# In-projection of a decoder layer: seven block products for eight, in two column groups

## What is computed

```python
x = layer_norm(...)                      # (1024, 1024)
u = x * (1.0 + sc2) + sh2
h = u @ w_in[l]                          # D_IN = 1976 columns
q_a, kc, vc, ksl, vsl, kwn, vwn, gate_logits, cq, ckv, k_rope = jnp.split(h, split_at, axis=-1)
```

## Time and profile before

| | |
|---|---|
| time, three executions | 2159.4, 2165.7, 2170.2 us; median 2165.7 |
| profiled execution | 2163.7 us, span from first to last instruction 2162.0 us |
| in-projection | first transpose at 693.6 us, last product starts at 886.5 us |
| TensorE busy in the span | 95% |
| mean granted TensorE clock | 0.983 of 2.4 GHz |

### The profile page before, as it was taken

One profiled execution on the slowest core, in us unless ns is written; L12 is line 12 of the kernel. 1 busy time (PEld: TensorE's weight loads), 2 busy tenths in 40 slices (PEclk: granted clock), 3 DMA queues, 4 the chain that ended last, 5 costly groups with the idle time before them and its releaser, 6 DMA issues. The chain is left out here.

```text
span 2162.0 us, 28296 instructions
## 1 busy us (share of the span) xinstructions
PE 2064.4 (95%) x10049; PEld 1725.5 (80%) x10049; DVE 1518.0 (70%) x2342; ACT 983.4 (45%) x1893; POOL 755.4 (35%) x702
## 2 busy tenths in 40 slices
PE   5999999999999999889998899999999999999997
PEld 4788888877887888778787888778888888878885
DVE  6877777868688523679988678765655555558689
ACT  3433233334644321578878467634533333234443
POOL 0366556620200000167555135401145655630201
PEclk9999999999998999999999999999999999999999
DMA  7254554457941332010000000042233233348975
GB/s 276 88 175 158 175 174 155 159 176 250 297 155 46 107 119 72 6 42 1 1 1 1 1 1 1 30 156 89 87 108 108 92 118 103 127 153 257 299 245 97
DMA packets 195710, 254.38 MB, mean 118 GB/s; under 512 B 20271, under 2 KB 118639, under 8 KB 195574
## 3 DMA queue, kind: packets, MB, share of 16 engines
q1 hardware_dynamic: 180166, 208.04, 29.0%
q0 software_dynamic: 15408, 44.57, 8.0%
HBM read 212.72 MB, written 43.52 MB: 119 GB/s over the span
## 5 line engine op out<-in xcount | busy, mean ns | idle before, releaser
L2993 POOL TENSOR_TENSOR nsa_exps<-nsa_exps,nsaa_factor 128x512 f32<-128x512 f32 (+1 forms) x102 | 96.3, 973 | 91.9 <-DVE nsaa_factor L2980 91.9
L758 DVE TENSOR_TENSOR ffn2A_u<-ffn2A_u,ffn_banks 128x512 f32<-128x512 f32 x60 | 41.2, 687 | 116.6 <-PE ffn_banks L702 112.5
L1292 DVE SCALAR_TENSOR_TENSOR late_part_late<-ada_rows,far_silu_c,late_part_late 128x1024 f32<-128x1024 f32 x56 | 107.1, 1912 | 3.4 <-DMA ada_rows<-in_w_ada 3.3
L579 ACT ACTIVATE ffn1A_t_hi<-ffn1A_t 128x512 fp32r<-128x512 f32 x80 | 48.5, 628 | 132.8 <-POOL ffn1A_t L572 102.9
L579 ACT ACTIVATE ffn2A_t_hi<-ffn2A_t 128x512 fp32r<-128x512 f32 x80 | 48.4, 628 | 122.8 <-POOL ffn2A_t L572 93.7
L702 PE MATMUL ffn_banks<-ffn1S_s_hi,ffn1A_t_hi 128*128 128x512 f32 x240 | 93.8, 391 | 0.0
L702 PE MATMUL ffn_banks<-ffn1S_s_hi,ffn1A_t_lo 128*128 128x512 f32 x240 | 93.4, 389 | 0.0
L702 PE MATMUL ffn_banks<-ffn1S_s_lo,ffn1A_t_hi 128*128 128x512 f32 x240 | 93.4, 389 | 0.0
L702 PE MATMUL ffn_banks<-ffn2S_s_hi,ffn2A_t_hi 128*128 128x512 f32 x240 | 93.4, 389 | 0.0
L702 PE MATMUL ffn_banks<-ffn2S_s_lo,ffn2A_t_hi 128*128 128x512 f32 x240 | 93.4, 389 | 0.0
L702 PE MATMUL ffn_banks<-ffn2S_s_hi,ffn2A_t_lo 128*128 128x512 f32 x240 | 93.4, 389 | 0.0
(11 more groups left out here) (660 smaller groups left out, 7034.6 us busy)
## 6 DMA issues: line engine op xcount, KB each, us to landing
ada_rows<-in_w_ada POOLq DMA_DIRECT2D x56, 512.0 KB, 4.7
ffn_raw_g<-in_ffn_wg SPq DMA_DIRECT2D x44, 512.0 KB, 3.7
ffn_raw_u<-in_ffn_wu SPq DMA_DIRECT2D x44, 512.0 KB, 5.0
early_w<-in_w_ada SPq DMA_DIRECT2D x16, 512.0 KB, 7.2
mix_in_w_raw<-in_w_in SPq DMA_DIRECT2D x32, 247.0 KB, 2.7
ffn_rest<-in_ffn_wd SPq DMA_DIRECT2D x29, 256.0 KB, 5.0
hidden<-ffn1A_c SPq DMA_DIRECT2D x22, 256.0 KB, 4.5
hidden<-ffn1A_u SPq DMA_DIRECT2D x22, 256.0 KB, 5.0
```

Source lines behind the costliest of these rows:

```text
L579: act.activation(self.b_hi[w][:, :], self.block_of(w), ACT.Copy).then_inc(self.rounded, 1)
L758: dve.tensor_tensor(out, base, bank, ALU.add).then_inc(self.mixed, 1)
L1292: dve.scalar_tensor_tensor(out=part_late[:, v, :], in0=ada[:, n % 2, :], scalar=silu_c[:, k:k + 1], in1=part_late[:, v, :], op0=ALU.mult, ...
L2993: pool.tensor_tensor(at, at, by, ALU.mult).then_inc(self.weighed, 1)
```

## The change

The product is cut into two column groups, 0 to 1303 (group 0) and 1304 to 1975 (group 1), and in each group rows, columns and depth are halved: 512 rows, 652 or 336 columns, depth 512. The four blocks of the result come from seven block products for eight. With a the four blocks of `u` and b those of the weight, the left operands are a11, a12, s1 = a21 + a22, s4 = a12 - s2, s2 = s1 - a11, s3 = a11 - a21, a22; the right ones are b11, b21, and differences of pieces. Products `m2`, `m3`, `m7`, `m4` go on in the banks of the product before them (`IN_JOINS`), which are read to `h` first and not cleared.

There are 14 stages (product, group), numbered 0 to 13, each of four chunks, numbered 0 to 55 through all stages: stage 0 is chunks 0 to 3. A group 0 chunk is 4 row tiles x 3 products x 2 halves of 326 columns; a group 1 chunk is 4 x 3 products of 336 columns. The weight pieces are 326 KB and 168 KB. There are four raw buffers (`RAWS`) and three slots of split weights (`PARTS`). `m5` loads two pieces a chunk and blends them once, `m6` three pieces and two blends, `m7` and `m4` one and one; all blends are GpSimd's. ScalarE reads the banks of stages 0 to 3, VectorE those of stages 4 to 13 and adds what is in `h`. The 64 one-column instructions of the modulation sums stand ahead of chunk 0. The residual rows, their stores, the 2 MB loads (`ahead`, in front of chunks 31 and 37) and the rotary rows are spread over the chunks. The diff, cut to its core:

```diff
+KH = DC // 2
+IN_GROUPS = ((0, COL_CQ // 2), (COL_CQ, (D_IN - COL_CQ) // 2))
+IN_STAGES = (("m1", 1), ("m2", 1), ("m1", 0), ("m2", 0), ("m5", 0), ("m3", 0), ("m5", 1), ("m3", 1),
+             ("m6", 0), ("m7", 0), ("m4", 0), ("m6", 1), ("m7", 1), ("m4", 1))
+IN_LEFT = {"m1": "a11", "m2": "a12", "m5": "s1", "m3": "s4", "m6": "s2", "m7": "s3", "m4": "a22"}
+IN_JOINS = ("m2", "m3", "m7", "m4")
+IN_PIECES = {"m1": ((0, 0),), "m2": ((1, 0),), "m5": ((0, 1), (0, 0)), "m3": ((1, 1),), "m6": ((1, 1), (0, 1), (0, 0)),
+             "m7": ((0, 0),), "m4": ((1, 0),)}
+IN_BLENDS = {"m1": 0, "m2": 0, "m5": 1, "m3": 0, "m6": 2, "m7": 1, "m4": 1}
+RAWS, PARTS = 4, 3
...
+        def piece_free(eng, r):
+            q, j = pieces[r]
+            name = chunks[q][1]
+            if name == "m6":
+                eng.wait_ge(blended, blends_before[q] + (1 if j == 1 else 2))
+            elif j == 1:
+                eng.wait_ge(blended, blends_before[q] + 1)
+            else:
+                eng.wait_ge(split, q + 1)
...
         @block.sync
+            def load(q):
+                _, name, g, c = chunks[q]
+                for j, (kh, nh) in enumerate(IN_PIECES[name]):
+                    r = piece_no[q, j]
+                    if r >= RAWS:
+                        piece_free(sp, r - RAWS)
+                    first = IN_GROUPS[g][0] + nh * width(g)
+                    sp.dma_start(piece(q, j), src[:, kh * KH + c, first:first + width(g)]).then_inc(landed[r % RAWS], 16)
...
+            for q in range(RAWS, len(chunks)):
...
+                for i in stores.get(q, ()):
+                    store(i)
+                if q == 31:
+                    sp.wait_ge(x_out, 16 * TT)
+                    ahead(sp, 0)
+                if q == 37:
+                    ahead(sp, 1)
+                load(q)
...
         @block.gpsimd
+            def mix(q):
+                _, name, g, c = chunks[q]
+                if not IN_BLENDS[name]:
+                    return
+                for j in range(len(IN_PIECES[name])):
+                    piece_landed(pool, q, j)
+                p0 = piece(q, 0)
...
+                elif name == "m6":
+                    pool.tensor_tensor(p0, p0, piece(q, 1), ALU.subtract).then_inc(blended, 1)
+                    if q == KH * in_stage("m6", 0):
+                        wait_used(pool, KH * in_stage("m5", 1) + KH - 1)
+                    pool.wait_ge(blended, blends_before[q] + 1)
+                    pool.tensor_tensor(t2(g, c), p0, piece(q, 2), ALU.add).then_inc(blended, 1)
...
         @block.scalar
+            def weight(q):
+                _, name, g, c = chunks[q]
+                if IN_BLENDS[name]:
+                    act.wait_ge(blended, blends_before[q + 1])
+                else:
+                    piece_landed(act, q, 0)
+                if q >= PARTS:
+                    wait_used(act, q - PARTS)
+                act.activation(b_hi[:, q % PARTS, 0:width(g)], product(q), ACT.Copy).then_inc(hi_ready, 1)
...
+            unit(8)
+            take(0)
+            unit(9)
...
+            unit(14)
+            unit(15)
+            weight(9)
+            take(1)
+            weight(10)
...
         @block.vector
+            grown_at = {15: 3, 17: 4, 20: 5, 21: 6, 23: 7}
+            rope_at = {39: (0,), 40: (1,), 43: (2,), 44: (3,), 47: (4,), 49: (5,), 51: (6,), 53: (7,)}
+            for q in range(11, len(chunks)):
+                if q >= KH * 4 + 6 and (q - 6) % KH == 0:
+                    take((q - 6) // KH)
+                if q in sums_at:
+                    sums(sums_at[q])
+                for name, c in low_at.get(q, ()):
+                    sum_low(name, c)
+                weight(q)
+                if q in grown_at:
+                    grow(grown_at[q])
+                for i in rope_at.get(q, ()):
+                    turn_rows(i)
+            take(len(IN_STAGES) - 1)
...
         @block.tensor
+            def rows(q):
+                n, name, g, c = chunks[q]
+                a = IN_LEFT[name]
+                pe.wait_ge(split, q + 1)
...
+                for t in range(KH):
+                    if c == 0:
+                        bank_free(n, t)
+                    tile = slice(t * P, (t + 1) * P)
+                    for m, (ua, wb) in enumerate(((0, b_hi), (0, b_lo), (1, b_hi))):
+                        for b in range(2 - g):
+                            bank, n_cols = (t, width(1)) if g else (2 * t + b, edge // 2)
+                            last = pe.matmul(acc[:, bank, 0:n_cols], part(a, ua, c)[:, tile],
+                                             wb[:, q % PARTS, b * n_cols:(b + 1) * n_cols],
+                                             start=(name not in IN_JOINS and c == 0 and m == 0), stop=(c == KH - 1 and m == 2),
+                                             skip_group_check=True)
```

More of the change, by code:

```diff
@@ new lines, in project_in @@
+        landed = [s.sem(f"landed{k}") for k in range(RAWS)]
+        blended, hi_ready, split, used, row_done = (s.sem(x) for x in ("blended", "hi_ready", "split", "used", "row_done"))
+        taken_act, taken_dve = s.sem("taken_act"), s.sem("taken_dve")
+        s1_made, s3_made, s2_made, s4_made = (s.sem(x) for x in ("s1_made", "s3_made", "s2_made", "s4_made"))
+        sum_hi, sum_split = s.sem("sum_hi"), s.sem("sum_split")
+        rows_in, scaled, grown = s.sem("rows_in"), s.sem("scaled"), s.sem("grown")
@@ L1891, in _, with rows_of, row_parts @@
+        def rows_of(i, cols, g):
+            at = out[:, i, cols]
+            return at.rearrange("p (b n) -> p b n", b=2) if g == 0 else at
+        def row_parts(i):
+            return x_sb[:, i, :].rearrange("p (b n) -> p b n", b=4)
+        row_gain, row_offset = (out[:, 4 * k:4 * k + 4, IN_GROUPS[1][0] + width(1):IN_GROUPS[1][0] + width(1) + D // 4] for k in range(2))
         @block.sync
         def _(sp):
[L1893 to L1910, removed]
@@ new lines, in _ @@
+            stores = {12: (0,), 13: (1,), 15: (2,), 20: (3,), 22: (4,), 25: (5,), 26: (6,), 28: (7,)}
+            for q in range(RAWS):
+                load(q)
+            sp.wait_ge(cols_summed, 1)
+            for place, rows in zip((row_gain, row_offset), norm_rows):
+                sp.dma_start(place, rows.rearrange("a (b n) -> a b n", b=4).to_broadcast([P, 4, D // 4])).then_inc(rows_in, 16)
+            for q in range(RAWS, len(chunks)):
+                if q == 12:
+                    sp.wait_ge(gate_made, 2)
+                    with nc.allow_non_contiguous_dma(reason="two gates, one column each chunk"):
+                        for v in range(2):
+                            sp.dma_start(gate_dram[v].rearrange("(c p) -> p c", p=P), gate[:, v, :]).then_inc(gate_out, 16)
+                for i in stores.get(q, ()):
[5 more added lines that the diff above has]
+                    ahead(sp, 1)
+                load(q)
@@ new lines, in _ @@
+            act.wait_ge(folded, 2)
+            for m in range(3):
+                unit(m)
+                weight(m)
+            unit(3)
+            weight(3)
+            unit(4)
+            unit(5)
+            weight(4)
+            unit(6)
+            unit(7)
+            weight(5)
+            unit(8)
+            take(0)
+            unit(9)
+            weight(6)
+            unit(10)
+            unit(11)
+            gates()
+            weight(7)
+            unit(12)
+            unit(13)
@@ L2008, in _ @@
-            later_blocks(dve, one)
+            for m in range(4):
+                unit(m)
+                weight(m)
+            unit(4)
+            unit(5)
+            weight(4)
+            unit(6)
+            unit(7)
+            weight(5)
+            weight(6)
+            masks.dve(dve)
+            weight(7)
+            grow(0)
+            weight(8)
+            grow(1)
+            weight(9)
+            weight(10)
+            grow(2)
+            grown_at = {15: 3, 17: 4, 20: 5, 21: 6, 23: 7}
@@ L2024, in sums_of @@
+            for m in range(3):
+                turn(m)
+            for at in range(4):
                 for cc in range(DC):
```

367 lines of the change are left out of this document (226 added, 141 removed).

## The result

The changed kernel takes 2204.5 us (median of 4 runs, 2202.5 to 2208.2), the kernel before 2166.0 beside it: ratio 1.018 (95% interval 1.015 to 1.021). The sign was right, the size was not: +17 us was forecast, +38.5 came, and 2204.5 is 3.5 us above the range.

What follows compares the result with a forecast made beforehand. TensorE, busy 95%, was taken as the bound. Terms -18.4 + 4.0 + 15.8 + 3.4 + 9.2 gave +14.0 us; clock 2 and contention 1 made +17, 2183 us; range 2167 to 2201.

Steps and rivals of the forecast that it cites:

- The sum for the in-projection: First transpose to last product: 193.3 us before, +14.0 from the summed terms, plus 2 for clock and 1 for contention.
- Products: In-projection: 672 products of 326 columns at 0.148 us and 336 of 336 at 0.152, 21.2 us less.
- Rival (b): Narrow products do not pay: each costs the 0.188 us a weight load shows, time 2222; chance 0.03.
- Opening: All 64 modulation sums ahead of the first product run at 1.2 GHz: 13.6 us for 8.9, +4.7.
- the second slow stretch: Half-clock stretch of 3.41 us behind the last sums should go, with a pause of 0.7: -1.9 us.
- m6: Wide m6 chunks: loads and two blends in series take 7.2 us against TensorE's 3.55; 15.8 us lost, mostly before stage 8.
- Rival (a): GpSimd stays ahead with m6's blends and the time is no slower, 2162; chance 0.19.
- VectorE's queues: Bank reads behind VectorE's other work: waits of 2.1 us before stage 5, 4.8 before stage 12, 2.4 before the last.
- Contention ... 0 to 5, I take 1: VectorE and GpSimd slow each other side by side, little in m6, more in the rotary rows; 1 us charged.
- Clock: The clock may fall in a wait, with half-rate products for up to 4.8 us after; 0 to 7 us, 2 charged.
- Rival (c): Clock stays low through stages 0 and 1 (+12) and every later wait restarts slow (+5): 2200; chance 0.07.
- The range's high end: Stretched blends 4.4 and 3 us, rotary rows 5, clock 7 on top of 14: +33, 2199; range reaches 2201.

Runs made afterwards that it cites:

- e13: Changed kernel in the best order of work found, without blends and their 24 further piece loads (block differences left out): 2153.3 us, ratio 0.994.
- e3: Changed kernel with m6's first blend started after two pieces and written into the sum's buffer, freeing both raw buffers: 2191.0 us, ratio 1.011.
- e2: Changed kernel with VectorE reading the banks of stages 7 and 8 before weights 33 and 37 instead of behind them: 2201.9 us, ratio 1.016.
- e6: Changed kernel with rotary rows 4 to 7 moved behind weights 46, 50, 51 and 54: 2197.0 us, ratio 1.015.
- e7: Changed kernel with residual rows 5 to 7 and the low parts of s3 moved behind the read of stage 4's banks: 2200.1 us, ratio 1.016.
- e5: e1 plus GpSimd subtractions of the blends' number and widths on a scratch place, awaited by nobody (block differences left out): 2174.7 us, ratio 1.005.
- e1: Changed kernel without blends, one piece a chunk and 24 loads fewer (block differences left out): 2165.1 us, ratio 1.000.

## Why the prediction missed, point by point

The sum for the in-projection was 193.3 + 14.0, + 2 clock, + 1 contention = 210.3 us; measured 231.4, 21.1 more.

- **Products, right but for 2.6 us.** 326 columns were 0.150 to 0.151 us apart and 336 0.153 to 0.155 for 0.148 and 0.152. Rival (b) is out. e13 shows what is left when nearly nobody is late: 692.6 to 875.1 us with 3.4 us of waits is 179.1 us of work, for 193.3 - 18.4 = 174.9 forecast. That is 4.2 more, 2.6 of it in the products.
- **Opening, right.** The first product came at 708.5 and the clock rose at 713.3, 4.8 us later; the second slow stretch was gone.
- **m6, right.** Loop 7.0 to 7.4 us for 7.2; 12.6 us before stage 8 for "about 14.6 to 27.5", then 2.0 before chunk 35: that is 14.6, and 15.5 with the 0.9 before chunk 31, for 15.8. Shortening the loop gave 13 us (e3), moving the read in front of m6 left chunk 35 where it was (e2). Rival (a) is out, as GpSimd waited for DMA in every round.
- **VectorE's queues, named rightly and mis-sized.** Before stage 5 5.3 us for 2.1, before stage 9 4.85 for 3.4, before stage 12 6.4 for 4.8, chunk 47 2.9 for 2.0, before stage 13 2.9 for 2.4, small ones in stages 1 to 4 3.5 for 1.9, before chunks 40 and 44 1.3 for none: with m6 42.6 for 32.4, 10.2 more. The places were right: e6 and e7 removed two of them by order alone.
- **The step that failed: "Contention ... 0 to 5, I take 1".** e5 measured 9.6 us without any blend being waited for. It works through these same waits; how much of the 10.2 it is in the changed kernel, where blends are also late, no run separates. I had read from the earlier trace rows that an operation grows from 0.69 to 1.24 us or from 1.29 to 1.74, and had argued that little meets in m6. But a VectorE operation on two SBUF operands that meets a blend waits for its end, however short it is itself. And the low halves and sums ahead of stage 5 meet the blends of m5, which I had called easily hidden. Here VectorE, then GpSimd, in the changed kernel:

```profile
757.59 1.21 DVE L2155 SCALAR_TENSOR_TENSOR early_x<-early_x,h_h 128x1024 f32<-128x1024 f32 x1
758.84 2.51 DVE L2157 SCALAR_TENSOR_TENSOR early_x<-h_h,early_x 128x1024 f32<-128x1024 f32 x1
761.27 2.68 DVE L2161 TENSOR_TENSOR mix_in_a<-h_h,mix_in_a 128x512 fp32r<-128x512 f32 x2
```

```profile
756.09 4.18 POOL L2010 TENSOR_TENSOR mix_in_w_raw<-mix_in_w_raw 128x652 f32<-128x652 f32 x1 [5.43 <-DMA mix_in_w_raw<-in_w_in]
760.68 2.13 POOL L2010 TENSOR_TENSOR mix_in_w_raw<-mix_in_w_raw 128x652 f32<-128x652 f32 x1 [0.41 <-DMA mix_in_w_raw<-in_w_in]
```

  2.51 for 1.22 us, 2.68 for 1.28, and a blend of 1.56 takes 4.18. From there I read a chain, which no run tested by itself: the late blends delay weights 16 and 17, their buffers come free late, weight 18 comes late, VectorE idles 2.3 us in front of it with its queue behind, and weight 20 is split at 776.6, though chunk 17 was done at 772.2.
- **Clock, also mis-sized: 2 for 7.6.** Chunks 20, 32, 36, 47 and 48 lasted 1.3 to 1.6 us longer than their neighbours, 7.6 in all with chunk 49. Rival (c) was right on this half: every wait of 2.85 us and more but the last (2.90, before stage 13) restarted slow. In e1 the waits of 2.1, 2.7 and 2.4 us were followed by half clock too (stretches from 783.5, 868.9 and 879.1 us), while 2.0 us before chunk 35 and the 2.90 were not: the length of a wait alone does not tell. The half of (c) on the opening, 12 of its 17 us, was wrong; that its 2200 lies nearest to the measured time is luck.
- **The rest.** 10.2 less the 1 already charged, 5.6 of clock and 4.2 of work are 19.0; 2.1 remain. Some 1.6 of them come with the waits: nine chunks that end in a wait which e13 does not have took, without that wait, 0.14 to 0.26 us more than their neighbours. Outside the in-projection the distance between the two profiled executions grew from 36.9 us at the first transposes of the sparse part to 41.5 at the end. In the other runs this drift was 0.2 to 5.1 us with no edit to that part. It was not studied.

The range's high end, 2199 to 2201, added stretched blends, rotary rows and clock. It had neither VectorE's sums and residual rows in stages 3 and 4, nor what a late weight holds up behind it, nor the 4.2 us of work. The miss is 3.5 us, less than the 4.2 us of work alone, so none of them can be named as the one reason.

## What to carry to other kernels

Before moving elementwise work to an idle GpSimd, count which operations of VectorE take two operands from SBUF and lie at the same time; charge a whole GpSimd instruction for each short one, not a share. When one term saves TensorE time by making others prepare its operands, work out the period of the preparation (loads that wait for buffers, plus blends) before its mean load, and test it by removing the preparation altogether: e1 and e13 bounded the change in two runs. A wait that shows at a bank read can belong to a loop elsewhere; moving the read tells them apart.

## What the hardware showed unasked

- A load of 2048 KB took 8.9 and 11.4 us to land where pieces were in flight at its issue, 7.9 before; three pieces of 326 KB issued together (at 827.3 to 828.2) took 3.1, 3.6 and 3.9 us.
- GpSimd is slowed by VectorE too: 4.18 us for a blend that takes 1.56 alone.
- Sums of one column, 64 of them in 13.65 us right ahead of the products, all ran at 1.2 GHz; the clock rose 4.8 us after the first product.
